# Tap adds of the gate block moved behind the seven products in the up projection of a gated MLP

## The chip, the cores and the metric

The kernel runs on one core of one Trainium2 chip. The metric is the device time of one execution in microseconds (us). PE is the matrix engine (TensorE), PEld its weight loads, DVE the vector engine, ACT the scalar engine, SP the engine whose queue issues nearly all DMAs.

## What is computed

Two decoder layers over 256 tokens of width 2048, all in float32. Each ends in a gated MLP with a causal convolution of width 3 between the up projection and the activation. The change lies in this MLP:

```python
def conv_ffn(h, w_up, conv_w, conv_b, w_down):
    u = causal_dwconv(h @ w_up, conv_w, conv_b)      # width 3, depthwise, causal
    gate, val = jnp.split(u, 2, axis=-1)             # 5632 channels each
    return (jax.nn.gelu(gate) * val) @ w_down
```

## The kernel before

**Splitting.** The kernel gets float32 accuracy out of three products: a weight chunk `raw` is rounded by ACT into `w_hi`, DVE subtracts to get `w_lo`, and PE multiplies x_hi by w_hi, x_hi by w_lo and x_lo by w_hi. A chunk is 256 rows by 512 columns of a weight matrix (512 KB, one DMA). In the plain form it takes 12 matmuls. `raw`, `w_hi` and `w_lo` are rings of four slots. SP loads chunk c when DVE has written `w_lo` of chunk c-4; ACT rounds chunk c when it has landed and PE has used chunk c-4; DVE follows ACT, PE follows DVE.

**Pairs.** The up projection of a layer has 11 pairs j = 0 to 10, each of a gate block and a value block of 512 channels. A pair has slots i = 0 to 15, one weight chunk in each; the text calls the chunk of slot i chunk i. Pairs 1 to 9 of each layer (18 in both layers, 2 to 9 in a hardware loop) are in a fast form: slots 6 and 7 are worked together in seven products of three matmuls each, 21 matmuls in place of 24, for which DVE first builds four differences of weights (`up_w`), ACT rounds them (`up_hi`) and DVE splits them (`up_lo`). Pair 10 is plain.

**Work behind a block.** A finished block passes through `mlp_post` stage by stage, a stage per slot; each of the three compute engines and SP runs its own fixed order of instructions. The gate block of pair j-1 has stages 8 to 15 in slots 0 to 7 of pair j, the value block of pair j-1 has stages 0 to 7 in slots 0 to 7 and stages 8 to 15 in slots 8 to 15 of pair j, and the gate block of pair j has its stages 0 to 7 in slots 8 to 15 of its own pair. The stages:

- 5: ACT scales the rows of the block in PSUM (L767, `rows_scaled`), DVE turns them into `cross` by two transposes (L1831, L1832, `acc_drained`).
- SP writes `cross` to `turn_line` in DRAM in four DMAs (`put`, L448), in slot 9 for the value block, slot 1 for the gate block, and reads it back turned into `h` (`fetch_up`, L465), in slot 11 for the value block and slot 3 for the gate block. There is one `cross` and one `h` for both blocks. Before it fetches, SP waits until the block before has left `h`:

```python
        def fetch_up(ph, j, half):
            before = 2 * PAIRS * ph.layer + 2 * j + half
            if not (isinstance(before, int) and before == 0):
                sp.wait_ge(conv_done, before)
            fetch(ph.m_up + 2 * j + half)
```

- 11: ACT waits for the fetch (`moved`) and writes the last tap of the convolution with its bias into `pad_g` or `pad_v` (L774). 12: ACT scales `h` by the middle tap into `tap_t` (L777). 13: ACT scales `h` by the first tap in place (L782).
- 13: DVE adds `tap_t` (L1838). 14: DVE adds `h` (L1844) and signals `conv_done`. These are the two tap adds.
- 15: ACT takes the gelu of the gate (L787), which waits for `conv_done`. For the value block DVE multiplies by the gate in stage 14 (L1850), and both split the product into `act` in stage 15 (L791, L1855).

In the fast pairs DVE also adds up the parts of the seven products: `up_add` parts 0 and 1 in slots 11 and 12, and part 2 (L1801), for the value block of the pair before, in slot 4. ACT's L767 of the value block waits for part 2.

**After the up projection** the down projection begins with plain chunks, and its slots 0 to 21 carry the last stages of pair 10 in the same way.

Of the kernel before, what the change touches and what calls it, by code (L numbers as in the profile page):

```python
# [33 lines left out]
KC = KT // CT  # L34
# [3 lines left out]
QUADS = P // SQ  # L38
# [48 lines left out]
             [(0, c) for c in range(KC - 2)] + [(0, UP_PAIR), (1, UP_PAIR), (0, KC - 2)] + [(1, c) for c in range(KC - 1)])  # L87
UP_FAST_AT = UP_CHUNKS[1].index((0, UP_PAIR))
UP_LAST = KC
UP_FOLD_AT = (11, 12, 4)  # L90
UP_COPY_AT = 10
UP_ONE, UP_FIVE, UP_SIX, UP_SEVEN = 2, 3, 6, 7

# [91 lines left out]
def build(nc, x_t, params, w_gates, rope, decay, rel_bias, identity,  # L185
# [112 lines left out]
    def sem(name):  # L298
        return nc.alloc_semaphore(name)
# [14 lines left out]
    put_out, moved, added = sem("put_out"), sem("moved"), sem("added")  # L314
# [74 lines left out]
    def by_quad(ap):  # L389
        return ap.rearrange("p (i n) -> p i n", i=QUADS)  # L390
# [16 lines left out]
    def chunk_end(q, c):  # L407

        return RING * q + c + 1
# [193 lines left out]
    def _(eng):  # L603
# [9 lines left out]
        def split(q, c):  # L613

            s, turn = c % RING, q + c // RING
            eng.wait_ge(landed[s], 16 * (turn + 1))
            if not (isinstance(turn, int) and turn == 0):

                eng.wait_ge(chunk_used, RING * (turn - 1) + s + 1)
            act_f(w_hi[:, s, :, :], raw[:, s, :, :], ACT.Copy).then_inc(hi_ready, 1)  # L620
# [102 lines left out]
        def up_round(f, q, c):  # L723

            s, turn = c % RING, q + c // RING
            eng.wait_ge(landed[s], 16 * (turn + 1))
            eng.wait_ge(chunk_used, RING * (turn - 1) + s + 1)
            act_f(w_hi[:, s, 1, :], raw[:, s, 1, :], ACT.Copy).then_inc(hi_ready, 1)
            if not (isinstance(f, int) and f == 0):
                eng.wait_ge(up_used, f)  # L730
            for e in range(2):
                eng.wait_ge(up_made, 2 * f + e + 1)
                act_f(up_hi[:, 2 * e:2 * e + 2, :], up_w[:, 2 * e:2 * e + 2, :], ACT.Copy).then_inc(up_rounded, 1)  # L733

        def up_pair(ph, j, fast, fast_last):

            q = ph.q_up + 4 * j
            for i in range(2 * KC):
                if fast and i == UP_FAST_AT + 1:
                    up_round(UP_FAST * ph.layer + j - 1, q, i)  # L740
                else:
                    split(q, i)
                if fast and i == UP_COPY_AT:
                    eng.wait_ge(up_used, UP_FAST * ph.layer + j)
                    act_f(up_part[:, 0, :], ps[:, UP_ONE, :], ACT.Copy).then_inc(up_copied, 1)
                c = i % KC
                if i < KC:
                    mlp_post(KC + c, ph, 0, j - 1, fast_last)
                    mlp_post(c, ph, 1, j - 1, fast_last)
                else:  # L750
                    mlp_post(KC + c, ph, 1, j - 1, fast_last)
                    mlp_post(c, ph, 0, j, fast)

        def mlp_post(stage, ph, half, j, fast):

            k = ph.layer * 2 * PAIRS + 2 * j + half
            pad = pad_v if half else pad_g
            if stage == 5:

                if fast:  # L760
                    eng.wait_ge(up_added, 2 * (UP_FAST * ph.layer + j - 1) + half + 1)
                else:
                    eng.wait_ge(chunk_used, chunk_end(ph.q_up + 4 * j + 2 * half, KC - 1))
                eng.wait_ge(rstd_ready, 2 * ph.layer + 2)
                for t in range(2):
                    row = ps[:, 4 * half + t, :]
                    ins = act_f(row, row, ACT.Copy, scale=rstd[:, S + t:S + t + 1])  # L767
                ins.then_inc(rows_scaled, 1)
            if stage == 11:
                eng.wait_ge(moved, 16 * (ph.m_up + 2 * j + half + 1))  # L770
                for t in range(BT):
                    w = conv_at(ph.layer, FFN_TAPS - 1, half, j, t)
                    b = conv_b_at(ph.layer, half, j, t)
                    act_f(by_quad(pad[:, t, 0:S]), h_tiles[:, :, t, :], ACT.Identity, scale=w, bias=b)  # L774
            if stage == 12:
                for t in range(BT):
                    ins = act_f(by_quad(tap_t[:, t, :]), h_tiles[:, :, t, :], ACT.Copy,  # L777
                                scale=conv_at(ph.layer, 1, half, j, t))
                ins.then_inc(tap_first, 1)
            if stage == 13:  # L780
                for t in range(BT):
                    ins = act_f(h_tiles[:, :, t, :], h_tiles[:, :, t, :], ACT.Copy,  # L782
                                scale=conv_at(ph.layer, 0, half, j, t))
                ins.then_inc(tap_last, 1)
            if stage == 15 and half == 0:
                eng.wait_ge(conv_done, k + 1)
                act_f(pad_g[:, :, 0:S], pad_g[:, :, 0:S], ACT.Gelu_apprx_tanh).then_inc(gelu_done, 1)  # L787
            if stage == 15 and half == 1:
                g = ph.layer * PAIRS + j
                eng.wait_ge(prod_ready, g + 1)  # L790
                act_f(act[:, bass.ds(j * BT, BT), 0, :], pad_v[:, :, 0:S], ACT.Copy).then_inc(act_hi, 1)  # L791

        def conv_at(layer, tap, half, j, t):
            base = PARAM_AT["ffn_conv_w"] + (layer * FFN_TAPS + tap) * 2 * FT + half * FT + t
            return par[:, bass.ds(base + j * BT, 1)]

        def conv_b_at(layer, half, j, t):
            base = PARAM_AT["ffn_conv_b"] + layer * 2 * FT + half * FT + t
            return par[:, bass.ds(base + j * BT, 1)]
# [157 lines left out]
        for ph in phases:  # L957
# [61 lines left out]
            with eng.Fori(2, UP_FAST + 1) as j:  # L1019
                up_pair(ph, j, True, True)  # L1020
# [389 lines left out]
    def _(eng):  # L1410
# [392 lines left out]
        def up_pair(ph, j, fast, fast_last):  # L1803

            q, f = ph.q_up + 4 * j, UP_FAST * ph.layer + j - 1
            for i in range(2 * KC):
                if fast and i == UP_FAST_AT:
                    up_diffs(f, q, i)
                if fast and i == UP_FAST_AT + 1:
                    up_lows(f, q, i)  # L1810
                else:
                    split(q, i)
                if fast and i in UP_FOLD_AT[:2]:
                    up_add(ph, j, UP_FOLD_AT.index(i))
                if fast_last and i == UP_FOLD_AT[2]:
                    up_add(ph, j - 1, 2)
                c = i % KC
                if i < KC:
                    mlp_post(KC + c, ph, 0, j - 1)
                    mlp_post(c, ph, 1, j - 1)  # L1820
                else:
                    mlp_post(KC + c, ph, 1, j - 1)
                    mlp_post(c, ph, 0, j)

        def mlp_post(stage, ph, half, j):
            n, k = ph.n_up + 2 * j + half, ph.layer * 2 * PAIRS + 2 * j + half
            pad = pad_v if half else pad_g
            if stage == 5:

                eng.wait_ge(rows_scaled, ph.scaled_up + 2 * j + half + 1)  # L1830
                step(v.transpose(flip_by_seq[:, 0], flip_from[:, 4 * half]))  # L1831
                v.transpose(flip_by_seq[:, 1], flip_from[:, 4 * half + 1]).then_inc(acc_drained, 1)  # L1832
                eng.wait_ge(acc_drained, n + 1)
            if stage == 13:

                eng.wait_ge(tap_first, k + 1)
                to = pad[:, :, 1:S + 1]
                step(tt(to, to, tap_t[:, :, :], ALU.add))  # L1838
            if stage == 14:

                eng.wait_ge(tap_last, k + 1)
                step.sync()
                to = pad[:, :, 2:S + 2].rearrange("p t (i n) -> p t i n", i=QUADS)
                tt(to, to, h_quads.rearrange("p i (t n) -> p t i n", t=BT), ALU.add).then_inc(conv_done, 1)  # L1844
                eng.wait_ge(conv_done, k + 1)
            if half and stage >= 14:
                g = ph.layer * PAIRS + j
                if stage == 14:
                    eng.wait_ge(gelu_done, g + 1)
                    tt(pad_v[:, :, 0:S], pad_v[:, :, 0:S], pad_g[:, :, 0:S], ALU.mult).then_inc(prod_ready, 1)  # L1850
                    eng.wait_ge(prod_ready, g + 1)
                if stage == 15:
                    eng.wait_ge(act_hi, g + 1)
                    tiles_j = bass.ds(j * BT, BT)
                    tt(act[:, tiles_j, 1, :], pad_v[:, :, 0:S], act[:, tiles_j, 0, :].bitcast(F32),  # L1855
                       ALU.subtract).then_inc(act_lo, 1)
                    eng.wait_ge(act_lo, g + 1)
# [470 lines left out]
```

## Time and profile before

| what | value |
|---|---|
| median of three runs | 2173.3 us (2173.15 to 2174.23) |
| profiled execution, its time | 2177.84 us |
| profiled execution, span | 2176.1 us |
| busy: PE, PEld | 100%, 83% of the span |
| busy: DVE, ACT | 78%, 63% of the span |
| mean DMA rate over the span | 230 GB/s |
| granted clock of PE | 1.0 in the mean |

Times in rows count from the start of the span. In a timeline row the second number is the time from the start of the first to the end of the last instruction of the row, and the bracket is how long the engine had sat idle and what ended the wait. Matmuls overlap: one of 128x512 is shown as 0.39 us long, but a new one starts every 0.227 us.

### The profile page before, as it was taken

To read this page: it belongs to the slowest core of one execution; us is meant where nothing else is said; L and a number is where in the kernel's file an instruction comes from. 1 tells how busy PE (TensorE), PEld (TensorE's weight loads), DVE (VectorE), ACT (ScalarE), POOL (GpSimd) and SP (SyncE) were. 2 spreads that over 40 slices of the span, in tenths; PEclk is the share of its full clock that TensorE was granted. 3 is DMA by queue.
4 is the path that set the end of the run, shared out by engine and by line. 5 is a ranking of instruction groups with operands and counts; after the bars stand their busy time and mean duration, and the time that the engine had idled before them with its cause. 6 is when DMAs were issued, how large, how long until landed. Compare 5 with 4: busy or idle time off the path is not lost.

```text
span 2176.1 us, 28498 instructions
## 1 busy us (share of the span) xinstructions
PE 2167.0 (100%) x9780; PEld 1795.9 (83%) x9780; DVE 1706.7 (78%) x1968; ACT 1360.0 (63%) x1950; POOL 16.6 (1%) x48
## 2 busy tenths in 40 slices
PE   9999999999999999999999999999999999999999
PEld 8888888887888888888888888888888888888887
DVE  7877866788888887887776676577888888878875
ACT  6654445677777777655555555556777777766553
POOL 2000000000000000000000000000000000000000
PEclk9999999999999999999999999999999999999999
DMA  8666667777777787666676777567877787777774
GB/s 276 218 210 211 200 191 242 218 236 239 246 248 239 245 253 237 208 223 213 228 245 201 233 263 242 186 220 217 257 229 253 229 255 232 257 237 217 238 246 156
DMA packets 269357, 500.15 MB, mean 230 GB/s; under 512 B 18928, under 2 KB 56832, under 8 KB 269136
## 3 DMA queue, kind: packets, MB, share of 16 engines
q1 hardware_dynamic: 267408, 492.78, 71.3%
q0 software_dynamic: 1424, 5.60, 0.7%
q8 instruction: 56, 0.92, 0.2%
q10 hardware_dynamic: 432, 0.56, 0.1%
q14 instruction: 37, 0.30, 0.0%
HBM read 457.15 MB, written 41.71 MB: 229 GB/s over the span
## 4 chain that ended last, share of the span: by engine, by line
PE 82%; DVE 7%; DMA 4%; ACT 3%; issue 3%; SPq 0%; ACTq 0%; DVEq 0%
PE ps L1186 16%; PE ps L1188 16%; PE ps L1187 16%; PE ps L1081 7%; PE ps L1083 7%; PE ps L1082 7%; PE ps L1058 4%; DMA h<-turn_line 2%; PE ps L1092 2%; PE ps L1094 2%; PE ps L1093 2%; DVE w_lo L1419 2%; PE ps L1062 2%; ACT w_hi L620 1%; DMA raw<-w_down 1%
## 5 line engine op out<-in xcount | busy, mean ns | idle before, releaser
L1419 DVE TENSOR_TENSOR w_lo<-raw,w_hi 128x1024 fp32r<-128x1024 f32 x744 | 897.9, 1222 | 347.2 <-ACT w_hi L620 334.6
L620 ACT ACTIVATE w_hi<-raw 128x1024 fp32r<-128x1024 f32 x744 | 770.9, 1053 | 441.4 <-PE ps L1188 165.2
L1186 PE MATMUL ps<-w_hi,xs 128*128 128x512 f32 x1904 | 743.2, 390 | 0.3 <-DVE w_lo L1419 0.3
L1187 PE MATMUL ps<-w_lo,xs 128*128 128x512 f32 x1904 | 740.8, 389 | 0.0
L1188 PE MATMUL ps<-w_hi,xs 128*128 128x512 f32 x1904 | 740.8, 389 | 0.0
L1186 PEld LDWEIGHTS ps<-w_hi,xs 128*128 128x128 f32 x1904 | 357.4, 188 | 75.7 <-DVE w_lo L1419 2.1
L1188 PEld LDWEIGHTS ps<-w_hi,xs 128*128 128x128 f32 x1904 | 357.4, 188 | 74.6
L1187 PEld LDWEIGHTS ps<-w_lo,xs 128*128 128x128 f32 x1904 | 357.5, 188 | 73.5
L1081 PE MATMUL ps<-w_hi,act 128*128 128x512 f32 x736 | 286.9, 390 | 0.4 <-DVE w_lo L1419 0.2
L1082 PE MATMUL ps<-w_lo,act 128*128 128x512 f32 x736 | 286.4, 389 | 0.0
L1083 PE MATMUL ps<-w_hi,act 128*128 128x512 f32 x736 | 286.4, 389 | 0.0
L1081 PEld LDWEIGHTS ps<-w_hi,act 128*128 128x128 f32 x736 | 138.1, 188 | 30.4 <-issue 1.1
L1083 PEld LDWEIGHTS ps<-w_hi,act 128*128 128x128 f32 x736 | 138.2, 188 | 28.9
L1082 PEld LDWEIGHTS ps<-w_lo,act 128*128 128x128 f32 x736 | 138.2, 188 | 28.4
L1058 PE MATMUL ps<-xs,w_hi 128*128 128x512 f32 x256 | 81.0, 397 | 2.2 <-DVE w_lo L1419 1.1
L782 ACT ACTIVATE h<-h,par 128x256 f32<-128x256 f32 x176 | 74.5, 494 | 0.0
L777 ACT ACTIVATE tap_t<-h,par 128x256 f32<-128x256 f32 x176 | 74.5, 494 | 0.0
L791 ACT ACTIVATE act<-pad_v 128x1024 f32 (+1 forms) x22 | 23.4, 1064 | 81.3 <-DVE pad_v L1850 81.3
L1062 PEld LDWEIGHTS ps<-xs,w_lo 128*128 128x128 f32 x256 | 48.1, 188 | 11.3
L767 ACT ACTIVATE ps<-ps,rstd 128x512 f32<-128x512 f32 x88 | 53.0, 633 | 0.0
L704 ACT ACTIVATE shared_hi<-shared_w 128x1024 fp32r<-128x1024 f32 x40 | 41.9, 1058 | 16.4 <-DVE shared_w L1626 7.7
L733 ACT ACTIVATE up_hi<-up_w 128x1024 fp32r<-128x1024 f32 x36 | 38.2, 1062 | 21.5 <-DVE up_w L1767 14.6
(312 smaller groups left out, 2004.8 us busy)
## 6 DMA issues: line engine op xcount, KB each, us to landing
raw<-w_up SPq DMA_DIRECT2D x352, 512.0 KB, 4.4
raw<-w_in SPq DMA_DIRECT2D x191, 512.0 KB, 4.5
raw<-w_down SPq DMA_DIRECT2D x176, 512.0 KB, 4.8
turn_line<-cross SPq DMA_DIRECT2D x284, 128.0 KB, 2.4
h<-turn_line SPq DMA_DIRECT2D x71, 512.0 KB, 5.3
raw<-w_out SPq DMA_DIRECT2D x64, 512.0 KB, 4.8
prob_line<-probs_t SPq DMA_DIRECT2D x12, 192.0 KB, 3.7
probs<-prob_line SPq DMA_DIRECT2D x3, 768.0 KB, 6.3
```

The lines of the kernel that those rows point to most:

```text
L620: act_f(w_hi[:, s, :, :], raw[:, s, :, :], ACT.Copy).then_inc(hi_ready, 1)
L777: ins = act_f(by_quad(tap_t[:, t, :]), h_tiles[:, :, t, :], ACT.Copy, scale=conv_at(ph.layer, 1, half, j, t))
L782: ins = act_f(h_tiles[:, :, t, :], h_tiles[:, :, t, :], ACT.Copy, scale=conv_at(ph.layer, 0, half, j, t))
L1058: return mm(ps[:, 4 * group + m, :], w_hi[:, s, u, m * P:(m + 1) * P], rhs, start=first and u == 0, stop=False)
L1062: return mm(ps[:, 4 * group + m, 0:S], w_lo[:, s, u, m * P:(m + 1) * P], rhs[:, 0:S], start=False, stop=last and u == CT - 1)
L1081: mm(out, x_hi, w_hi[:, s, u, :], start=first and u == 0, stop=False)
L1082: mm(out, x_hi, w_lo[:, s, u, :], start=False, stop=False)
L1083: ins = mm(out, x_lo, w_hi[:, s, u, :], start=False, stop=last and u == CT - 1)
L1186: mm(out, x_hi, w_hi[:, s, u, :], start=first and u == 0 and not (begun and t == 0), stop=False)
L1187: mm(out, x_hi, w_lo[:, s, u, :], start=False, stop=False)
L1188: ins = mm(out, x_lo, w_hi[:, s, u, :], start=False, stop=last and u == CT - 1)
L1419: tt(w_lo[:, s, :, :], raw[:, s, :, :], w_hi[:, s, :, :].bitcast(F32), ALU.subtract).then_inc(lo_ready, 1)
```

## The change

Both tap adds of a gate block go to stages 16 and 17, that is from slots 5 and 6 to slots 8 and 9, behind the seven products' slots; its gelu goes from stage 15 to stage 18 (slot 7 to slot 10). The value block's tap adds stay where they are. `up_add` part 2 goes from slot 4 to slot 3. DVE's turning of a value block gets a wait of its own until the four writes of the gate block's `cross` are done, since the add that came before it implied this until now. SP's program is not changed.

```diff
-UP_FOLD_AT = (11, 12, 4)
+UP_FOLD_AT = (11, 12, 3)
+TAP_ADDS, GELU_AT = ((16, 17), (13, 14)), 18
...
@@ scalar, up_pair @@
                 else:
+                    mlp_post(2 * KC + c, ph, 0, j - 1, fast_last)
                     mlp_post(KC + c, ph, 1, j - 1, fast_last)
                     mlp_post(c, ph, 0, j, fast)
...
-            if stage == 15 and half == 0:
+            if stage == GELU_AT and half == 0:
                 eng.wait_ge(conv_done, k + 1)
...
@@ vector, up_pair @@
                 else:
+                    mlp_post(2 * KC + c, ph, 0, j - 1)
                     mlp_post(KC + c, ph, 1, j - 1)
                     mlp_post(c, ph, 0, j)
...
@@ vector, mlp_post @@
                 eng.wait_ge(rows_scaled, ph.scaled_up + 2 * j + half + 1)
+                if half:
+                    eng.wait_ge(put_out, 16 * QUADS * (ph.m_up + 2 * j + half))
...
-            if stage == 13:
+            if stage == TAP_ADDS[half][0]:
...
-            if stage == 14:
+            if stage == TAP_ADDS[half][1]:
```

## Rows read from the trace of the kernel before

**Rows 1.** The page's busy times of the engines.

```profile
PE 2167.0 (100%) x9780; PEld 1795.9 (83%) x9780; DVE 1706.7 (78%) x1968; ACT 1360.0 (63%) x1950; POOL 16.6 (1%) x48
```

**Rows 2.** Waits of PE, then the waits for up_lo: us in total, times.

```profile
PE ps L1092 <- DVE up_lo L1782: 0.7, 4, 0.2
...
  PEld ps L1092: 4.6, 11
```

**Rows 3.** One pair of the loop by windows: busy us of each engine, clock, DMA.

```profile
611.90:654.80 42.90, 42.90 (x190) 35.34 (x189) 37.61 (x37) 32.60 (x50) 0.00 (x0) 1.00 0.79 244
```

**Rows 4.** Timeline of DVE in slots 5 to 11 of that pair.

```profile
605.04 1.22 DVE L1838 TENSOR_TENSOR pad_g<-pad_g,tap_t 128x1024 f32<-128x1024 f32 x1
606.61 0.72 DVE L1831 STREAM_TRANSPOSE cross<-ps 128x512 f32<-128x512 f32 x1 [0.34 <-ACT ps L767]
...
610.96 1.23 DVE L1419 TENSOR_TENSOR w_lo<-raw,w_hi 128x1024 fp32r<-128x1024 f32 x1
612.10 1.22 DVE L1844 TENSOR_TENSOR pad_g<-pad_g,h 128x1024 f32<-128x1024 f32 x1
613.44 0.69 DVE L1778 TENSOR_TENSOR w_lo<-raw,w_hi 128x512 fp32r<-128x512 f32 x1
614.05 2.36 DVE L1782 TENSOR_TENSOR up_lo<-up_w,up_hi 128x1024 fp32r<-128x1024 f32 x2
616.32 4.87 DVE L1419 TENSOR_TENSOR w_lo<-raw,w_hi 128x1024 fp32r<-128x1024 f32 x4
```

**Rows 5.** Timeline of ACT in slots 7 to 11 of that pair.

```profile
613.35 1.06 ACT L787 ACTIVATE pad_g<-pad_g 128x1024 f32<-128x1024 f32 x1 [1.42 <-DVE pad_g L1844]
...
618.38 0.60 ACT L745 ACTIVATE up_part<-ps 128x512 f32<-128x512 f32 x1 [1.12 <-PE ps L1094]
...
620.48 2.08 ACT L774 ACTIVATE pad_v<-h,par 128x256 f32<-128x256 f32 x4 [0.55 <-DMA h<-turn_line]
```

**Rows 6.** Timeline of SP's queue in that pair (issues, not transfers).

```profile
612.35 2.34 SPq L428 DMA_DIRECT2D raw<-w_up  x2
614.90 0.35 SPq L465 DMA_DIRECT2D h<-turn_line  x1
617.71 11.13 SPq L428 DMA_DIRECT2D raw<-w_up  x6
...
636.46 0.37 SPq L465 DMA_DIRECT2D h<-turn_line  x1
```

**Rows 7.** Issue to landing: six fetches (L465, 560 to 700 us), the page's loads.

```profile
DMA to landing us min/median/max: 4.6/4.9/5.4
...
raw<-w_up SPq DMA_DIRECT2D x352, 512.0 KB, 4.4
```

**Rows 8.** Timeline of DVE: slots 12, 15 and next 0.

```profile
623.54 1.23 DVE L1419 TENSOR_TENSOR w_lo<-raw,w_hi 128x1024 fp32r<-128x1024 f32 x1 [1.04 <-ACT w_hi L620]
...
634.53 1.23 DVE L1419 TENSOR_TENSOR w_lo<-raw,w_hi 128x1024 fp32r<-128x1024 f32 x1
...
637.54 3.50 DVE L1419 TENSOR_TENSOR w_lo<-raw,w_hi 128x1024 fp32r<-128x1024 f32 x3 [0.54 <-ACT w_hi L620]
```

**Rows 9.** Timeline of PE: first matmuls of slots 6, 12 and next 0.

```profile
613.27 0.39 PE L1092 MATMUL ps<-w_hi,xs 128*128 128x512 f32 x1
...
629.06 0.39 PE L1186 MATMUL ps<-w_hi,xs 128*128 128x512 f32 x1
...
639.94 0.39 PE L1186 MATMUL ps<-w_hi,xs 128*128 128x512 f32 x1
```

**Rows 10.** The down projection of layer 0: timelines of SP, ACT, DVE and PE.

```profile
870.49 0.34 SPq L465 DMA_DIRECT2D h<-turn_line  x1
...
878.34 0.58 ACT L774 ACTIVATE pad_v<-h,par 128x256 f32<-128x256 f32 x1
...
894.67 1.22 DVE L1419 TENSOR_TENSOR w_lo<-raw,w_hi 128x1024 fp32r<-128x1024 f32 x1
...
896.16 0.40 PE L1081 MATMUL ps<-w_hi,act 128*128 128x512 f32 x1
```

## The prediction

> **What bounds the kernel now.** First the page's busy times: PE is busy for the whole span, DVE for 78% and ACT for 63% [rows 1]. A faster DVE or ACT is therefore worth only what PE still waits for. The list of PE's waits comes next. In the seven products PE itself waited 0.7 us for `up_lo`, and the weight loads for them waited 4.6 us in 11 cases, part of which lies under the matmul in flight [rows 2]. Over the 18 fast pairs I take 3 us of this as what the change could give back (between 0.7 and 5.3). Then the windows: a pair in the loop takes 42.90 us, all of it PE, at full granted clock (the 2.4 GHz level), with DVE busy for 37.6 of them [rows 3]. 189 matmuls at one per 0.227 us are 42.9 us too, so inside the pair there is next to nothing to gain.
>
> What matters is then how far DVE and ACT are ahead of PE, slot by slot, in this one pair, since the order of work is fixed by hand and repeats. PE begins the products at 613.27, slot 12 at 629.06 and the next pair's slot 0 at 639.94 [rows 9]; slots between are 12 x 0.227 = 2.72 us apart. DVE ends the `w_lo` that these need at 624.77 for slot 12, 635.76 for slot 15 and 638.77 for next 0 (the first of the three in that row) [rows 8]. PE starts slot 15 at 637.22, so the lead is 4.3, then 1.5, then 1.2 us. It shrinks because DVE's steps from slot to slot take (635.76 - 624.77) / 3 = 3.7 us and then 3.0, filled with adds and turnings, against PE's 2.72. Anything that makes slot 12 late by more than 1.2 us reaches PE by the next pair's slot 0.
>
> **The change part by part.**
>
> *The adds leave slots 5 and 6.* The first one [rows 4] ended 0.34 us before DVE's turning could begin, which waited for ACT; without it that wait is about 1.5 us and the turning starts at the same time. The second add is 1.22 us long, with pitch and wait 1.26 us, between `w_lo` of slot 6 and that of slot 7 (612.10 to 613.44). `up_lo` comes that much earlier, 615.1 in place of 616.4 for the second half. That takes away the waits of rows 2, about 3 us in all.
>
> *The adds enter slots 8 and 9.* DVE's work is the same in sum, so its busy time stays. In time order, at the pitch of 1.14 us of the row of four `w_lo` [rows 4]: `up_lo` ends at 615.1, `w_lo` 8 at 616.3, first add 617.4, `w_lo` 9 618.6, second add 619.8. `conv_done` thus comes at 619.8 in place of 613.3, 6.5 us later. `w_lo` 10 and 11 end near 621 and 622, where PE needs them at 623.6 and 626.3: no loss there.
>
> *The gelu.* It waited 1.42 us on ACT [rows 5]. ACT is now free to round slots 8 and 9 earlier, and in slot 10 it waits until about 619.8 for `conv_done`, behind the copy of `up_part` that ends at 618.98 [rows 5]. Slot 11 is rounded near 622, and PE needs it at 626.3. Its result is wanted only by the product of slot 14. Nothing on the path.
>
> *`up_add` part 2 in slot 3.* It needs PE's chunk 15 of the pair before. ACT may round chunk 3 only when PE has used that same chunk 15 (the ring has four slots), and DVE comes to the add behind `w_lo` 3, so it finds PE done. It costs nothing; without that cover DVE would wait for PE, and each us of it would come off the lead of slot 4.
>
> *The wait for `put_out`.* The gate's fetch itself waits for these writes; it went out at 636.46 less one pair, so at 593.6 [rows 6], and the value block's turning starts at 606.61 [rows 4]. DVE finds it fulfilled; a wait instruction is below 0.1 us and lies in the wait for ACT.
>
> *What the text of the change does not show: SP.* The fetch of the value block into `h` waits for the gate block's `conv_done`, since `h` is the one that the gate's second add reads. Before, that signal stood at 613.3, and SP reached the fetch at 614.9, right behind the loads of slots 10 and 11 [rows 6]. Now the fetch waits until 619.8, and is issued near 619.9, 5.0 us later. Queued behind it on SP are the loads of slots 12, 13 and so on. Slot 12's load was issued at 617.71 and would now be issued near 620.4; with the loads' median of 4.4 us to landing [rows 7] it lands near 625. The fetch takes 4.6 to 5.4 us to land, median 4.9 [rows 7]; I take 4.8, as no load is in flight ahead of it. It lands at 624.7.
>
> ACT waits for it. Before, ACT began the tap of `pad_v` at 620.48, and even so it waited 0.55 us for that DMA [rows 5]: the old fetch had no slack. Now it begins at 624.8, 4.3 us late, and everything behind it on ACT is late by the same: the rounding of slot 12, so DVE's `w_lo` 12, so the chain of rows 8, in which DVE has no idle time until slot 15 is done. Slot 12 alone has 4.3 us of lead and barely stalls; by the next slot 0 the lead is 1.2, so PE stalls 4.3 - 1.2 = 3.1 us in the first pair of a layer, spread over slots 13 to next 0: three steps of 3.7 - 2.72 = 1.0 (less rounding) and one of 0.3.
>
> In the pairs that follow it is more. DVE and ACT leave slot 15 4.3 us late, PE 3.1: they begin the pair 1.2 us nearer to PE. The gate's fetch, issued at 636.46 behind slot 3's load [rows 6], lands just when ACT can use it, and shifts by this 1.2 as well, so ACT's slots 3 to 5, the turning, the differences and `conv_done` are each 1.2 us late against PE. `w_lo` 6 (612.18, lead 1.1) costs 0.1 to 0.3 there, and the value fetch is later by the rest, 0.9 to 1.1. Per pair this makes 3.1 + 1.2 = 4.3; some small gaps between DVE's instructions (the 0.54 at the loop's end [rows 8] among them) can close in a chain that runs late, so I take 4.0.
>
> DMA: Bandwidth & Descriptors of the Trainium skill, section "Anatomy of one DMA — SWDGE (gpsimd) path", fits the time of a DMA as 2.0 us and the bytes at 436 GB/s, for another issuing path than SP's. For 512 KB that gives an estimate of 3.2 us, 1.6 us below what the fetches here show, and the first pair's stall would be 1.5 us in place of 3.1. The traces of the fetches decide, and the sum goes by them.
>
> *Pair 10 and the down projection.* Pair 10 is plain: DVE has none of the seven products' work (`up_lo` alone is 2.36 us [rows 4], and differences and `up_add` come on top), so it absorbs the late fetch; I put 0, and the bound is the 3.1 of a first pair. In the down projection the last gate's adds move from slots 5 and 6 to 8 and 9 too. The value fetch goes from 870.49 to about 875.4 by the same order of DVE, ACT's tap from 878.34 to about 880.3, 1.9 us late. DVE ended `w_lo` of slot 15 at 895.89 and PE began that slot at 896.16 [rows 10], so there is no lead and all of it counts: 1.9 x 2 layers = 4 us.
>
> **The sum.** First fast pairs 2 x 3.1 = 6; the other fast pairs 16 x 4.0 = 64; down projections 4; given back at the seven products 3. Together +71 us on the profiled execution's 2177.84 (its span is 2176.1, 1.7 less), that is 2249. That execution is 4.5 us (0.2%) above the median 2173.3, and the runs are to be forecast: 2173.3 + 71 = 2244, I say 2245.
>
> Bounds of the one unknown, the fetch's landing and what follows from it: with 4.6 us and the small gaps absorbed 3.2 per pair, so about 57 - 3 = +54; if the fetch alone, without its neighbours, were 1 us faster than any shown, 2.2 per pair, +38 (2211). With 5.4 us and the carry-over doubled by it, 5.3 per pair, +100 (2273).
>
> **The rivals.**
>
> *The late fetch stays under cover* (the other side). The four-slot ring gives slack, and then only the 3 us at the seven products are seen: 2170. For it speaks the 4.3 us of lead in slot 12; against it the 1.2 us at the next slot 0 and the 0.55 us that ACT waited already. It decides if the new fetch delays ACT's tap by less than 1.2 us, so if it landed within 1.8 us of its issue, where none took less than 4.6. Chance 3 in 100, two of them within 0.2%.
>
> *A part of it only.* The fetch lands faster than any shown, or DVE catches up in slots 13 to 15: 1.5 to 2.4 us per pair, 2198 to 2214. The skill's estimate above falls here. Against it: DVE's work there leaves no gap to catch up in but the 0.54 us of the loop's end [rows 8]. 12 in 100.
>
> *More than that.* The fetch and the loads of slots 12 to 15 now go out within some 3 us, where they were spread over 7. If the weights themselves land late, or the fetch takes longer than 5.4, each further 1 us costs up to 2 us per pair: beyond 2273. For it: the mean rate in this pair is 244 GB/s with the DMA engines busy 0.79 of the time [rows 3], so bursts have little room. 10 in 100.
>
> *The forecast*: 75 in 100. That the adds are not moved at all cannot be: they are plain program order.
>
> **The numbers.** The time is the forecast's, 2245. The forecast and the near parts of its two neighbours make the range 2212 to 2275. About 0.2% (4 us) is what a measurement of this kernel can tell from no change: faster by more 1%, within it 2 to 3%, slower by more 96%.
>
> **What would show it.** In the profile after: the fetch of the value block (L465) is issued about 5 us later against the pair's products, and SP's own waits list `pad_g` of the gate's second add; ACT's `pad_v` tap waits 3 to 5 us for `h<-turn_line`, 18 times; PE waits for `w_lo` 60 to 80 us in all, in slots 12 to 0; a pair takes 46 to 47.5 us in place of 42.90; the waits for `up_lo` are gone or small; busy times of DVE and ACT in us are unchanged. It is wrong if ACT's wait for `h` is short, or if PE's waits are elsewhere, at the seven products or at slots 10 and 11.

## The result and the profile after

The changed kernel takes 2237.86 us (median of 4, 2235.07 to 2240.49), the one before 2173.49. The ratio is 1.0296, with a 95% interval of 1.0278 to 1.0313: slower by 64 us. The forecast was 2245, with a range of 2212 to 2275.

The page of the profile after, its busy times [rows 1]:

```profile
PE 2187.3 (98%) x9780; PEld 1791.2 (80%) x9780; DVE 1704.0 (76%) x1968; ACT 1360.8 (61%) x1950; POOL 16.6 (1%) x48
```

DVE and ACT are as busy in us as before: no work was added for them. The list of PE's waits [rows 2]:

```profile
PE ps L1188 <- DVE w_lo L1421: 36.4, 57, 0.9
PE ps L1083 <- DVE w_lo L1421: 2.9, 3, 1.4
PE ps L1094 <- DVE w_lo L1421: 2.4, 6, 0.7
```

SP's own waits:

```profile
SPq L465 <- DVE pad_g L1849: 98.1, 16, 6.1
...
SPq L466 <- DVE pad_g L1849: 33.3, 6, 6.3
```

The wait for `up_lo` (L1782 before) is gone from the list, which is what the change was to buy. SP waits 22 times for the gate's second add, L1849: that row did not exist before. The reader has to know that PE's waits (42.6 us for `w_lo` in all) understate the loss: the end of a matmul is modelled, and a stall counts only from there. The windows show the loss itself. The same pair as in [rows 3], by windows:

```profile
622.73:669.76 47.03, 44.36 (x190) 35.01 (x189) 37.71 (x37) 32.83 (x50) 0.00 (x0) 1.00 0.68 222
```

47.03 us in place of 42.90, with the same 190 matmuls, the same work on DVE and ACT, and full granted clock. The loss is at these places in PE's timeline (start of the products first, then where slots 12 to 15 and the next 0 begin; compare [rows 9]):

```profile
624.11 0.39 PE L1094 MATMUL ps<-w_hi,xs 128*128 128x512 f32 x1
...
640.67 0.50 PE L1188 MATMUL ps<-w_hi,xs 128*128 128x512 f32 x1 [0.73 <-DVE w_lo L1421]
...
644.20 0.50 PE L1188 MATMUL ps<-w_hi,xs 128*128 128x512 f32 x1 [0.52 <-DVE w_lo L1421]
...
647.92 0.50 PE L1188 MATMUL ps<-w_hi,xs 128*128 128x512 f32 x1 [0.70 <-DVE w_lo L1421]
...
651.66 0.50 PE L1188 MATMUL ps<-w_hi,xs 128*128 128x512 f32 x1 [0.72 <-DVE w_lo L1421]
...
654.67 0.50 PE L1188 MATMUL ps<-w_hi,xs 128*128 128x512 f32 x1
```

The steps are 3.53, 3.72, 3.74 and 3.01 us where PE needs 2.72: it runs at DVE's pace. These steps lose 3.1 us (0.8 + 1.0 + 1.0 + 0.3). Ahead of slot 12 it is 0.8 (640.67 - 624.11 is 16.56, before it was 15.79), and between the next slot 0 and the next products some 0.2. That is the pair's 4.1 us.

Upstream, the queue of SP [rows 6] in the timeline:

```profile
624.12 1.05 SPq L429 DMA_DIRECT2D raw<-w_up  x2
631.48 0.35 SPq L466 DMA_DIRECT2D h<-turn_line  x1
632.12 3.09 SPq L429 DMA_DIRECT2D raw<-w_up  x4
```

The landing of the fetches between 560 and 760 us [rows 7]:

```profile
DMA to landing us min/median/max: 3.3/3.9/4.6
```

ACT in the timeline [rows 5]:

```profile
631.40 1.06 ACT L789 ACTIVATE pad_g<-pad_g 128x1024 f32<-128x1024 f32 x1 [1.69 <-DVE pad_g L1849]
632.36 1.04 ACT L621 ACTIVATE w_hi<-raw 128x1024 fp32r<-128x1024 f32 x1
634.95 2.08 ACT L776 ACTIVATE pad_v<-h,par 128x256 f32<-128x256 f32 x4 [1.54 <-DMA h<-turn_line]
638.30 1.06 ACT L621 ACTIVATE w_hi<-raw 128x1024 fp32r<-128x1024 f32 x1 [1.27 <-DMA raw<-w_up]
```

Counted from the start of the products, the fetch goes out at 7.37 us (before 1.63), ACT's tap starts at 10.84 (before 7.21), and slot 12 is rounded at 14.19 (before 9.19: the tap's start and its 1.98 us to the next instruction). The fetch lands 3.3 us after its issue, and the tap starts 0.2 us behind that; no fetch of the kernel before landed as fast. But then ACT waits 1.27 us more, for the weights of slot 12, which the blocked queue held back too: issued at 632.12, they land 6.1 us later. That second wait was not forecast. It is over 0.4 us in 9 of the 17 fast pairs behind the very first; in the mean of the 17, ACT's idle time there is 0.66 us.

DVE's chain [rows 4, 8] is close to where it was forecast. The second add ends 7.25 us after the start of the products (forecast: 6.5, and 0.9 to 1.1 more in a pair behind a first one):

```profile
626.74 1.22 DVE L1421 TENSOR_TENSOR w_lo<-raw,w_hi 128x1024 fp32r<-128x1024 f32 x1
627.87 1.22 DVE L1843 TENSOR_TENSOR pad_g<-pad_g,tap_t 128x1024 f32<-128x1024 f32 x1
629.01 1.22 DVE L1421 TENSOR_TENSOR w_lo<-raw,w_hi 128x1024 fp32r<-128x1024 f32 x1
630.14 1.22 DVE L1849 TENSOR_TENSOR pad_g<-pad_g,h 128x1024 f32<-128x1024 f32 x1
...
639.39 1.23 DVE L1421 TENSOR_TENSOR w_lo<-raw,w_hi 128x1024 fp32r<-128x1024 f32 x1 [3.40 <-ACT w_hi L621]
```

### The profile page after: what moved, and what is told of

It is laid out like the page before. It is cut to its first block, busy times and chain, and to the rows that moved or that the text cites. A ratio compares the mean times of both kernels' runs of the same rounds, so it can differ in the third digit from the quotient of the medians.

```text
span 2235.7 us, 28520 instructions
## 1 busy us (share of the span) xinstructions
PE 2187.3 (98%) x9780; PEld 1791.2 (80%) x9780; DVE 1704.0 (76%) x1968; ACT 1360.8 (61%) x1950; POOL 16.6 (1%) x48
## 4 chain that ended last, share of the span: by engine, by line
PE 55%; DVE 19%; DMA 9%; issue 9%; ACT 7%; SPq 1%; ACTq 1%; DVEq 0%
PE ps L1188 9%; PE ps L1189 9%; PE ps L1190 9%; PE ps L1083 6%; PE ps L1085 6%; PE ps L1084 6%; DVE w_lo L1421 6%; DMA h<-turn_line 4%; PE ps L1060 4%; DMA raw<-w_up 3%; ACT w_hi L621 3%; PE ps L1064 2%; DMA raw<-w_down 2%; ACT h L784 1%; DVE pad_v L1855 1%
## 5 line engine op out<-in xcount | busy, mean ns | idle before, releaser
L776 ACT ACTIVATE pad_v<-h,par 128x256 f32<-128x256 f32 x88 | 45.8, 592 | 29.0 <-DMA h<-turn_line 29.0
L1836 DVE STREAM_TRANSPOSE cross<-ps 128x512 f32<-128x512 f32 x44 | 31.4, 714 | 35.0 <-ACT ps L769 35.0
```

## The experiments

Two questions: is it the late signal (the theory on record) and not the crowding of DVE in slots 8 and 9 or another part of the edit; and what exactly is late behind the signal, the fetch of `h` or the loads queued behind it. All runs were compared with the kernel before on the same chip; its median there was 2175.7 to 2177.8. "Late signal" is the theory on record: the cost comes from `conv_done`, for which SP's fetch waits.

### Everything but the adds

```diff
-TAP_ADDS, GELU_AT = ((16, 17), (13, 14)), 18
+TAP_ADDS, GELU_AT = ((13, 14), (13, 14)), 18
```

> Everything of the change but the move of the two tap adds: up_add part 2 in slot 3, the gelu in slot 10, the wait for put_out before the value block's turning; the gate's tap adds stay in slots 5 and 6. Late signal (the theory on record: the cost comes from conv_done, for which SP's fetch of h waits): within 0.2% of before, 2169 to 2178 us. If the gelu's place, the fold's place or the added wait had a part in the loss: above 2180.

2187.77 us, ratio 1.0051 (1.0035 to 1.0068). The late-signal theory had everything else cost nothing; it costs half a per cent. At least one of the three small parts has a price of its own.

### The gelu alone

```diff
@@ the kernel before @@
-            if stage == 15 and half == 0:
+            if stage == GELU_AT and half == 0:      # GELU_AT = 18
                 eng.wait_ge(conv_done, k + 1)
...
+                    mlp_post(2 * KC + c, ph, 0, j - 1, fast_last)
                     mlp_post(KC + c, ph, 1, j - 1, fast_last)
```

> The kernel before with one edit: the gate's gelu in slot 10 (stage 18) in place of slot 7. Gelu theory (from the profile of the kernel with everything but the adds: in slot 10 the gelu's 1.06 us stand right ahead of slot 11's rounding and pad_v's tap, in slot 7 they stood where ACT waited for PE anyway): slower by 0.4 to 0.7%, as that kernel was. Rival, the fold in slot 3 or the wait for put_out made that loss: within 0.2% of before.

2185.28 us, ratio 1.0039 (1.0024 to 1.0054): it is the gelu. ACT in this kernel:

```profile
663.54 0.60 ACT L746 ACTIVATE up_part<-ps 128x512 f32<-128x512 f32 x1 [1.25 <-PE ps L1096]
664.04 1.05 ACT L789 ACTIVATE pad_g<-pad_g 128x1024 f32<-128x1024 f32 x1
664.99 1.05 ACT L621 ACTIVATE w_hi<-raw 128x1024 fp32r<-128x1024 f32 x1
665.94 2.07 ACT L776 ACTIVATE pad_v<-h,par 128x256 f32<-128x256 f32 x4
```

In slot 7 the gelu [rows 5] took time in which ACT would otherwise have waited; in slot 10 it stands behind the copy that waits for PE and ahead of slot 11's rounding and the tap, with no wait between. The tap starts 7.9 us after the products' start in this pair, 8.2 in the mean, in place of 7.2 and 7.3. In the first fast pair of a layer the gelu takes a load of ACT's function table along (ACT_TABLE_LOAD, 1.28 us, right ahead of it in both kernels): these two pairs take 43.46 and 43.89 us in place of 42.84.

### The gelu in slot 14

The same edit with `GELU_AT = 22`.

> The kernel before with the gate's gelu in slot 14 (stage 22), where ACT has 3.8 us of idle time ahead of the value block's last rounding. Gelu theory: no loss, within 0.2% of before or up to 0.2% faster. Rival, any later gelu costs: slower by 0.3% and more.

2177.21 us, ratio 1.0000 (0.9991 to 1.0009). It is the place in slot 10 that costs, not the delay of the gelu.

### The changed kernel with the gelu in slot 14

> The changed kernel with the gelu in slot 14 in place of slot 10. In the changed kernel ACT waits 1.3 us per pair for h and 1.3 for the weights of slot 12 after the gelu, so the gelu's 1.06 us are hidden there: the same as the changed kernel, 2233 to 2241 us. If the gelu adds to the loss as it does alone: 2225 to 2231 us.

2236.70 us, ratio 1.0267 (1.0246 to 1.0288), the changed kernel's being 1.0296 (1.0278 to 1.0313). The ratios differ by 0.0029, with 0.0027 either way, so these times alone leave room for up to 12 us that are the gelu's. The traces say less: from pair 1 to pair 9 a fast pair takes 46.25 us in place of 46.29, and the tap starts at the same place, 10.78 us after the products' start in the mean against 10.77. The gelu's time is hidden ahead of the wait for `h`, which grows to 4.1 us in the mean, as expected. In the pairs of the changed kernel the gelu's price does not come on top of the signal's.

### The two adds swapped

The adds stay in slots 8 and 9; the one that reads `h` comes first and has a signal for SP. Which add is done in which slot is all that differs, DVE's load is the same.

```diff
@@ sync, fetch_up @@
+            if half:
+                sp.wait_ge(h_read, PAIRS * ph.layer + j + 1)
+            elif not (isinstance(before, int) and before == 0):
                 sp.wait_ge(conv_done, before)
...
@@ vector, mlp_post @@
+            if half == 0 and stage == TAP_ADDS[0][0]:
+                eng.wait_ge(tap_last, k + 1)
+                to = pad[:, :, 2:S + 2].rearrange("p t (i n) -> p t i n", i=QUADS)
+                tt(to, to, h_quads.rearrange("p i (t n) -> p t i n", t=BT), ALU.add).then_inc(h_read, 1)
+            if half == 0 and stage == TAP_ADDS[0][1]:
+                eng.wait_ge(h_read, PAIRS * ph.layer + j + 1)
+                eng.wait_ge(tap_first, k + 1)
+                to = pad[:, :, 1:S + 1]
+                tt(to, to, tap_t[:, :, :], ALU.add).then_inc(conv_done, 1)
                eng.wait_ge(conv_done, k + 1)
...
```

> The changed kernel, with the two adds of the gate in the same slots 8 and 9, but the one that reads h first and signalled to SP by itself; DVE's work is the same in every slot, only the signal for the fetch of h comes one slot (some 2.3 us) earlier. Late signal: 2.3 us less delay, so about 2.3 us less per pair in 18 pairs, 2193 to 2203 us in place of 2238. Rival, DVE crowded in slots 8 and 9 (the adds themselves make w_lo late): no change, 2233 to 2243.

2197.29 us, ratio 1.0099 (1.0082 to 1.0116). A signal some 2.2 us earlier takes 41 us off, two thirds of the loss, with the same work in the same slots. Crowding in slots 8 and 9 is refuted as the cause of that part. ACT here never waits for `h`: the tap follows the gelu and slot 11 without a gap, so part of what is left is probably the gelu's. No kernel here shows that share alone; the one below with the second add in slot 8 has the signal about as early and the gelu in slot 14, and its ratio is 1.0058 (below), against 1.0099.

### The signal in steps

Three kernels with the first add in slot 5 and the gelu in slot 14, which differ only in the slot of the second add: `TAP_ADDS, GELU_AT = ((13, n), (13, 14)), 22` with n = 15, 16 and 17.

> The changed kernel with the gate's first add back in slot 5, the second in slot 7 behind up_lo (before the change: slot 6), and the gelu in slot 14. conv_done comes near 616.4 in the frame of the kernel before (before 613.3, changed 619.8), the fetch goes out 1.6 us later than before and the load of slot 12 not at all later. Late-signal theory: the cost is nearly gone (1.6 us of delay against 1.2 of lead, some 0.4 per pair at most) and the waits for up_lo and the halved w_lo are gone: 2168 to 2180 us. Rival, the adds' move out of slots 5 and 6 costs in itself: above 2190.

> A step on the scale of the late signal: the first add in slot 5, the second in slot 8 (after its w_lo), the gelu in slot 14. conv_done near 617.4 in the frame of the kernel before, 1.1 us later than with the second add in slot 7 (which took the time of before) and 2.4 earlier than in the changed kernel. Late signal: each us of delay beyond the lead costs 1.0 to 1.3 us per fast pair, so 2183 to 2197 us. Rival, a switch-like effect of leaving slots 5 to 7: the same as with slot 7, or the full loss.

> The next step: the first add in slot 5, the second in slot 9, the gelu in slot 14. conv_done near 618.6, 1.2 us earlier than in the changed kernel. Late signal: 2203 to 2222 us, between the one with slot 8 and the changed kernel (2238). If the place of the first add has no part in the loss and only the second one's slot counts: the full 2238.

Slot 7: 2175.63 us, ratio 0.9997 (0.9988 to 1.0006). Slot 8: 2191.18, 1.0058 (1.0036 to 1.0080). Slot 9: 2212.92, 1.0158 (1.0138 to 1.0177). All three are within what was expected of the late signal, and there is no switch: the first slot of delay costs nothing, the second 0.6% and the third 1.0%. In the kernel with slot 7 the fetch goes out 3.35 us after the products' start in place of 1.73 (means), and yet the tap is not late, as this fetch lands faster (the nearest load ahead of it went out 3.3 us earlier, in the kernel before 0.6 us):

```profile
659.13 0.35 SPq L466 DMA_DIRECT2D h<-turn_line  x1
```

```profile
662.58 2.09 ACT L776 ACTIVATE pad_v<-h,par 128x256 f32<-128x256 f32 x4 [0.33 <-DMA h<-turn_line]
```

3.45 us from issue to tap, where the kernel before took 5.6. This kernel also has what the change aimed at, no wait for `up_lo`, and is not measurably faster for it. None of the kernels here beats the one before.

### The load of slot 12 held alone

```diff
@@ the kernel before, up_loads: load() of slot 12 waits for w_lo of two slots more @@
-                sp.wait_ge(lo_ready, RING * (turn - 1) + s + 1)
+                sp.wait_ge(lo_ready, RING * (turn - 1) + s + 1 + held)      # held = 2 in slot 12, else 0
```

> The kernel before, with only the load of slot 12 held until w_lo of slot 10 is written (in place of slot 8), so about 2.3 us later, as the blocked fetch holds it in the changed kernel; the fetch of h is not touched. Fetch theory (what is late is h in ACT's pad_v tap): within 0.2% of before. Load theory (what is late is the weights of slot 12, which the profile after shows landing 6.2 us after their issue, 1.3 us after ACT was through with h): 0.8 to 2.5 us per fast pair, 2188 to 2218 us.

2199.34 us, ratio 1.0103 (1.0086 to 1.0120), as the load theory has it. The loads of slots 13 and 14 stand behind this one on SP's queue, so they cannot go out before it either. ACT:

```profile
668.31 2.08 ACT L774 ACTIVATE pad_v<-h,par 128x256 f32<-128x256 f32 x4
672.05 1.06 ACT L620 ACTIVATE w_hi<-raw 128x1024 fp32r<-128x1024 f32 x1 [1.66 <-DMA raw<-w_up]
```

The tap is nearly in time (7.85 us in the mean, before 7.32), and slot 12's rounding waits for its weights in all 18 fast pairs. A held load is enough to bring a loss by itself.

### The fetch late alone

```diff
@@ the kernel before, up_loads and the down projection @@
-                if i % KC == 3:
-                    fetch_up(ph, j - 1, i // KC)
+                if i in FETCH_AT:                                # FETCH_AT = (3, 13)
+                    fetch_up(ph, j - 1, FETCH_AT.index(i))
```

> The kernel before, with the value block's fetch of h issued behind the load of slot 13 in place of slot 11, so about 4.4 us later, while no load is held. Fetch theory: pad_v's tap is 2.3 to 3.7 us late, less the lead of 1.2: 1.1 to 2.5 us per fast pair, 2193 to 2220 us. Load theory: little, 2173 to 2180 us.

The median is 2277.2 us, ratio 1.0462 (1.0441 to 1.0483); three of four executions took 2273 to 2278, the fourth stands at 7811.5, which nothing here explains. The direction is the fetch theory's, the size more than twice its upper end. SP and ACT:

```profile
638.82 0.35 SPq L466 DMA_DIRECT2D h<-turn_line  x1
```

```profile
645.39 2.08 ACT L775 ACTIVATE pad_v<-h,par 128x256 f32<-128x256 f32 x4 [5.95 <-DMA h<-turn_line]
```

6.6 us from issue to tap, 6.4 of them to landing (5.5 to 6.4 in all 18 fast pairs), behind two loads that went out 1.7 and 0.6 us ahead, where I had counted 3.5 to 4.9; and I left out of the expectation the carry-over into the next pair that the prediction had. The tap starts 13.07 us after the products' start in the mean (before 7.32), 5.75 late.

### The fetch behind slot 12's load

The edit above in the changed kernel, with `FETCH_AT = (3, 12)`.

> The changed kernel with the value block's fetch of h issued behind the load of slot 12 in place of ahead of it; the signal it waits for is unchanged. Load theory alone (the load of slot 12 sets the end): its weights come 3 to 4 us earlier, 1.3 us less per pair, 2210 to 2220 us. Both are needed and share one queue (h now lands later by about what the load gains): the same as the changed kernel or up to 1 us per pair slower, 2232 to 2255 us.

2227.49 us, ratio 1.0231 (1.0216 to 1.0247) against the changed kernel's 1.0296: about 0.65%, 14 us less. It lies between the two expectations. ACT:

```profile
679.38 2.08 ACT L777 ACTIVATE pad_v<-h,par 128x256 f32<-128x256 f32 x4 [1.51 <-DMA h<-turn_line]
681.36 1.04 ACT L622 ACTIVATE w_hi<-raw 128x1024 fp32r<-128x1024 f32 x1
```

The wait for slot 12's weights is gone in every pair, and the fetch, against what I expected, lands no later after its issue (3.3 us in the mean in either kernel). The mean wait removed is 0.62 us over the 18 fast pairs, 11 us in all, and what was gained is 14 with 5 either way. I had taken the 1.27 us of one pair for all of them.

### All of them on one scale

When ACT rounds slot 12 is what most of these kernels have in common, whatever made it late. Mean over the 17 fast pairs behind the very first, from the timelines, counted from the first matmul of the products. The last column is (median - median before on the same chip) / 18; it charges the whole difference to the fast pairs and is good to 0.2 or 0.3 us:

| kernel | fetch issued | tap starts | slot 12 rounded | us per fast pair |
|---|---|---|---|---|
| before | 1.73 | 7.32 | 9.31 | 0 |
| gelu in slot 14 | 1.74 | 7.28 | 9.26 | 0 |
| gelu in slot 10 | 2.14 | 8.21 | 10.18 | 0.5 |
| everything but the adds | 2.15 | 8.19 | 10.16 | 0.6 |
| second add in slot 7 | 3.35 | 6.80 | 9.27 | 0 |
| second add in slot 8 | 4.98 | 8.39 | 10.95 | 0.9 |
| adds swapped | 5.11 | 9.27 | 11.28 | 1.1 |
| load of slot 12 held | 2.48 | 7.85 | 11.44 | 1.2 |
| second add in slot 9 | 6.25 | 9.69 | 12.32 | 2.1 |
| change, fetch behind load 12 | 7.38 | 10.83 | 12.82 | 2.8 |
| change, gelu in slot 14 | 7.37 | 10.78 | 13.47 | 3.4 |
| the change | 7.28 | 10.77 | 13.49 | 3.6 |
| fetch late alone | 7.02 | 13.07 | 15.06 | 5.5 |

From the kernel with the second add in slot 8 on, the rounding of slot 12 less 9.3 less a lead of about 0.9 is near the loss: 0.8, 1.1, 1.2, 2.1, 2.6, 3.3, 3.3 and 4.9, against the last column. The lead is fitted to these kernels; the one pair of the trace before gave 1.2.

The two kernels with the gelu in slot 10 and both adds in place do not lie on this scale: it gives them nothing, and they lose 0.5 and 0.6. Their PE does not stall in slots 8 to 15 in the pairs behind a layer's first; it stalls in the seven products of the next pair, by 0.8 us a pair where the kernel before stalls 0.4 and the change 0.1. The list of PE's waits with the gelu in slot 10 alone has it [rows 2 has 0.7 us, 4 times]:

```profile
PE ps L1094 <- DVE up_lo L1784: 2.5, 15, 0.2
```

So there are two places where ACT's delay reaches PE. The kernels with the second add still in slot 6, ahead of `w_lo` of slot 7, lose 0.8 to 1.1 us a pair in the products when ACT is late (1.1 with the load of slot 12 held, 1.1 with the fetch late alone). Those with the add moved lose 0.1 there and the rest behind the products. That a late ACT reaches the next pair's products is the reading that fits these stalls; no kernel here tests it by itself.

## Why the prediction was right

**The place and the mechanism.** `conv_done` was forecast 6.5 us after the start of the products in a first pair and 0.9 to 1.1 more in the others; it comes at 5.9 in the first pairs and at 7.1 to 7.4 in the others. That SP's fetch waits for it, that ACT waits for the fetch, and that PE then goes at DVE's pace through slots 12 to next 0 in steps of 1.0, 1.0, 1.0 and 0.3 is in the rows after (0.8, 1.0, 1.0, 0.3). The swapped adds show the cause by taking back a part of the signal's delay and nothing else; the three steps show its size slot by slot.

**The signs that were named.** The fetch goes out 5.5 us later in the mean, SP waits for `pad_g`, a pair takes 46.6 us, the waits for `up_lo` are gone, and the busy times are the same. Two signs are not as they were written. PE's listed waits for `w_lo` are 42.6 us in all, where 60 to 80 were forecast. And ACT's tap waits 1.4 us for `h` in the mean of the 18 pairs, not 3 to 5, which the prediction had called a sign against itself. It is none: in the pair shown ACT had already waited 1.69 us for the same signal at the gelu, which left 1.54 for the tap, and with the gelu out of the way (slot 14) the tap waits 4.1 in the mean.

**The size per pair.** 4.0 us were forecast for the pairs behind a first one, above 42.85 of pure work. From the products' start in pair 1 to that in pair 9 the change takes 370.1 us in layer 0 and 370.5 in layer 1 (before 345.1 and 346.0). Without the first interval (43.70 and 44.06) the other seven take 46.6 on average, 3.8 above pure work. The kernel before takes 43.2 there, so the difference is 3.4. The term was right in sum, and off inside. The fetch's landing was taken as 4.8 us and is 3.3: all six fetches of [rows 7] went out 0.5 to 0.6 us behind a load, so they did not speak for a fetch with nothing ahead of it. The trace before had a hint of it: the one of its fetches whose nearest load ahead was 4.6 us old (at 1205.38) landed in 3.7. And the loads held behind the fetch, which I had put as landing in time (4.4 us, near 625), go out in a burst; slot 12's takes 4.2 to 6.3 us and costs 0.66 on average. The errors do not cancel: the fetch takes 1.5 off, the load puts back less than half of it, and a lead nearer to 0.9 than to 1.2 some 0.3 more.

That the time still came out within 0.3% is in part luck. By the prediction's own bound a fetch 1 us faster than any shown makes 2.2 per pair and 2211 us, the low edge of its range. The fetch was 1.3 faster, which by the same steps is an estimate of 1.9 per pair and some 2208. A wait that it had put at nothing, a lead smaller than it had read and a profiled execution 4.4 us above its median brought the time back into place. That the held load costs by itself, and how much it costs in the change, is shown by the kernels with load 12 held and with the fetch behind it.

**First pairs.** 3.1 us each were forecast, 0.9 and 1.2 came (43.70 and 44.06 less 42.84). There the fetch went out at 5.9 us, not 6.6, and landed in 3.3, so the tap began at 9.25 and slot 12 was rounded at 11.24, 2.0 late against the pair of [rows 5], less the lead. This is 4 us less for both layers. The 16 later pairs were forecast at 4.0, less their part of the 3 given back, so at 3.8, and came at 3.4 (14 of them measured): some 7 us less. The two are nearly all of what lies between +71 and the 59.6 by which the two profiled spans differ. At the end of each layer, from pair 9's products of layer 0 to pair 1's of layer 1, the change takes 4.3 us more, and from pair 9's of layer 1 to the end 6.0. Pair 9's own stall of some 3.4 is contained in each; what is left, 3.5 for both layers, fits the 4 forecast for the down projections, which were not measured apart.

**The time before.** The sum was put on the median and not on the profiled execution. The profiled execution of the change took 2237.49, in the middle of its runs, that of the kernel before was 4.4 above its median: so the runs differ by 64.4 and the profiles by 59.6. The forecast of 2245 is 7 us above the time that came; against the profiles alone it is 11 too much.

**The bounds.** They do not follow from their own steps: 18 pairs at 3.2, 2.2 and 5.3 us, with 4 more for the down projections and 3 given back, make +59, +41 and +96, where the text has +54, +38 and +100. By these steps the bound of 2211 is 2214.

**The parts put at nothing.** `up_add` in slot 3 and the wait for `put_out` cost nothing that is measured (1.0051 with them and the gelu, 1.0039 with the gelu alone, intervals overlapping). The gelu was put at "nothing on the path". In the changed kernel that holds: moving it away changes the tap's start by 0.01 us. But the reason named, that its result is wanted late, was too short: in the kernel without the late signal the same move costs 0.4%. It is hidden only behind the larger loss.

**What is given back.** The wait for `up_lo` is gone, which was forecast with 3 us. By the starts of the matmuls PE lost 0.36 us in the products of each of the 16 later pairs before and loses 0.07 in the change, so 4.6 in all. The kernel with the second add in slot 7 has this gift without the loss, but the interval of its ratio (0.9988 to 1.0006) allows for at most 2.6 us in the whole time.

**The rivals.** That the late fetch stays under cover is so for a delay of 1.6 us at the issue, as the kernel with slot 7 shows, and not for the 5.5 of the change. A partial loss was to come if the fetch landed faster than any shown. It did, and the loss was still 3.4 per pair; a smaller one (0.9 and 1.2) came in the first pairs alone. "More than that" was to come from the burst of loads; the burst is real and cost 0.66 per pair, where some 1.8 was needed to pass 2273.

DMA: Bandwidth & Descriptors of the Trainium skill, section "Anatomy of one DMA — SWDGE (gpsimd) path", gave an estimate of 3.2 us for 512 KB. The trace agrees with it for a fetch with nothing ahead of it (3.3 in the pair shown), and not for one behind two loads (6.4) or a load behind a fetch (6.1). I had decided against it on fetches that all had loads in flight ahead.

## What to carry to other kernels

Before work is moved, list who waits for its signal, on every queue, and what is queued behind the waiting instruction there: here the adds were harmless where they went, and the price was on SP, whose program the diff does not touch. In a pipeline with a fixed order read the lead at each slot, not at the first one: 4.3 us of cover in slot 12 were 1.2 by the next slot 0, and what is late beyond the smallest lead is lost in every turn of the loop. And if a step is moved off a place where its engine would have waited anyway, it may cost where it lands, even with its consumer far away: the gelu's 1.06 us made the tap 0.9 us late and cost some 0.5 us per pair.

## What the runs showed that was not expected

In the change the value block's fetch of 512 KB goes out with no load in flight ahead of it and lands in 3.2 to 3.5 us in 17 of the 18 fast pairs (4.2 in one). Behind two loads of 512 KB that went out 0.6 and 2.5 us ahead, as in the kernel before, it takes 4.9 to 6.6, and behind two that went out 0.6 and 1.7 us ahead 5.5 to 6.4. One load that went out 3.3 us or more ahead hardly matters, though it is not yet down: with the second add in slot 7 the fetch lands in 3.3 us in the mean, and with the fetch put behind slot 12's load, which went out 3.4 us ahead, in 3.3 too (675.94 to the tap at 679.38). The load issued 0.6 us behind the fetch and followed by three more within 3 us takes 6.1 in the pair shown; why it takes 6.0 to 6.3 in seven fast pairs and 4.2 to 5.4 in the other eleven, these runs do not show. The order of fetch and load in SP's queue was worth 0.65% in the changed kernel, and a landing time read from one state of the queue did not carry over to another.
